# Two weight loads of the last expert split into 112 rows and two times eight rows

## What is computed

```
xe = h[idx]                                   # 16 experts x 32 tokens x 2048
hid = silu(xe @ w_gate) * (xe @ w_up)         # w_gate, w_up: 16 x 2048 x 1024
ye = (hid @ w_down) * gates                   # w_down: 16 x 1024 x 2048
h_lat = h_lat + mod * combine(idx, ye)        # then the final RMS norm
```

## Time and profile before

| | |
|---|---|
| median of three runs | 1685.66 us |
| the profiled execution | 1684.07 us |
| its span, first to last instruction | 1682.1 us |
| busy share of the span: PE, DVE, ACT, POOL | 86%, 42%, 19%, 7% |
| mean rate of the DMA engines over the span | 352 GB/s |
| chain that ended last | PE 57%, DMA 35%, DVE 4% |

### The profile page before, as it was taken

How to read it: one execution, slowest core, us unless ns; L and a number is a source line. 1 busy time by engine, 2 the same in 40 slices (tenths; PEclk the granted TensorE clock), 3 DMA queues, 4 the chain that set the end, 5 groups by cost and what they waited for, 6 DMA issues and landing times.

```text
span 1682.1 us, 19830 instructions
## 1 busy us (share of the span) xinstructions
PE 1451.6 (86%) x8030; PEld 867.9 (52%) x8030; DVE 712.0 (42%) x1149; ACT 327.7 (19%) x572; POOL 121.9 (7%) x106
## 2 busy tenths in 40 slices
PE   8999999999999998989878787766787776886786
PEld 6678778878888777875313241221332132332232
DVE  4446777678767876662222122112221211411122
ACT  3333333233333345530000000000000000000001
POOL 0000000004322243001000000000000000000002
PEclk8999999999999999999978888888888878878899
DMA  9996658657746764599999999999999999999997
GB/s 397 420 421 234 230 200 300 225 206 253 266 144 257 271 229 175 184 416 428 428 425 429 428 427 428 427 428 429 416 415 428 428 427 428 427 427 429 427 427 293
DMA packets 55404, 592.00 MB, mean 352 GB/s; under 512 B 6284, under 2 KB 6412, under 8 KB 7576
## 3 DMA queue, kind: packets, MB, share of 16 engines
q1 hardware_dynamic: 54008, 584.61, 85.0%
q10 hardware_dynamic: 1312, 6.16, 1.0%
HBM read 588.65 MB, written 2.10 MB: 351 GB/s over the span
## 4 chain that ended last, share of the span: by engine, by line
PE 57%; DMA 35%; DVE 4%; issue 2%; ACT 1%; POOL 0%; SPq 0%; DVEq 0%; POOLq 0%; ACTq 0%
DMA ring<-in_w_up 18%; DMA ring<-in_w_down 15%; PE bank L630 8%; PE bank L632 8%; PE bank L631 8%; PE bank L981 6%; PE bank L917 4%; PE bank L626 3%; PE bank L627 2%; PE bank L896 2%; PE bank L628 2%; PE bank L950 2%; PE bank L580 2%; PE bank L884 2%; DMA ring<-in_w_down_last 2%
## 5 line engine op out<-in xcount | busy, mean ns | idle before, releaser
L981 PE MATMUL bank<-ring,xg 128*32 128x512 f32 x1504 | 217.7, 707 | 122.5 <-DMA ring<-in_w_up 90.5
L1414 DVE TENSOR_TENSOR whl<-ring,whl 128x512 fp32r<-128x512 f32 x276 | 208.6, 759 | 131.1 <-ACT whl L1081 130.2
L1081 ACT ACTIVATE whl<-ring 128x512 fp32r<-128x512 f32 x276 | 173.4, 630 | 266.9 <-PE bank L632 219.4
L630 PE MATMUL bank<-whl,uh 128*128 128x512 f32 x512 | 206.5, 403 | 1.6 <-DVE vv L1443 0.7
L632 PE MATMUL bank<-whl,ul 128*128 128x512 f32 x512 | 199.8, 390 | 0.0
L631 PE MATMUL bank<-whl,uh 128*128 128x512 f32 x512 | 199.5, 390 | 0.0
L981 PEld LDWEIGHTS bank<-ring,xg 128*32 128x32 f32 x1504 | 45.0, 119 | 273.8 <-DMA ring<-in_w_up 140.7
L1397 DVE SCALAR_TENSOR_TENSOR part<-ring,csT,part 128x1024 f32<-128x1024 f32 x104 | 140.5, 1351 | 0.1
L896 PE MATMUL bank<-yy,gcur 128*128 128x512 f32 x252 | 132.9, 654 | 4.9 <-DVE yy L1708 3.5
L1280 ACT ACTIVATE gup<-bank 128x512 f32<-128x512 f32 x32 | 18.7, 597 | 593.5 <-PE bank L981 593.5
L1760 DVE COPY gup<-bank 128x512 f32<-128x512 f32 x32 | 22.0, 689 | 238.4 <-PE bank L981 238.4
(11 more groups left out here) (264 smaller groups left out, 1625.5 us busy)
## 6 DMA issues: line engine op xcount, KB each, us to landing
ring<-in_w_up SPq DMA_DIRECT2D x61, 2048.0 KB, 25.7
ring<-in_w_gate SPq DMA_DIRECT2D x33, 2048.0 KB, 25.7
ring<-in_w_mod_b SPq DMA_DIRECT2D x63, 1024.0 KB, 5.1
ring<-in_w_down SPq DMA_DIRECT2D x30, 2048.0 KB, 27.3
ring<-in_w_in SPq DMA_DIRECT2D x53, 1024.0 KB, 4.9
ring_b<-in_w_gate SPq DMA_DIRECT2D x15, 2048.0 KB, 20.5
ring_c<-in_w_gate SPq DMA_DIRECT2D x15, 2048.0 KB, 23.7
ring<-in_w_mod_a SPq DMA_DIRECT2D x28, 1024.0 KB, 16.1
```

The lines of the kernel that those rows point to most:

```text
L630: mm(ps, hi[:, k, cols], wh, start=k == 0, stop=False)
L981: last = mm(bank[2 * m + half][32 * kk:32 * kk + 32, :], xg[:, 4 * j + kk, CAP * ei:CAP * ei + CAP], parts[kk // of][0][:, kk % of, 512 * ...
L1081: a(whl[:, cidx % (AHEAD + 1), 0, :], slot_buf(slot[n])[:, 512 * (k % 4):512 * (k % 4) + 512], ACT.Copy).then_inc(hi_split, 1)
L1414: v.tensor_tensor(whl[:, cidx % (AHEAD + 1), 1, :], slot_buf(slot[n])[:, 512 * (k % 4):512 * (k % 4) + 512], whl[:, cidx % (AHEAD + 1), 0, ...
```

## The change

Items 6 and 7 of the last expert are no longer one transfer of 128 rows each. Each is issued as three transfers behind one wait: rows 0 to 111, rows 112 to 119, rows 120 to 127. All three add 16 to the semaphore of the same buffer, and the count that TensorE waits for before it uses the item is 32 higher. The bytes, their places in memory and the sources are the same.

```diff
+SHARED_ROWS = ((0, 112), (112, 120), (120, 128))
...
-        return pair_buf(d), ring_full[2 * d], g * (16 * 8) + (fills[2 * d] + 16 * (2 * ei + n // RING + 1))
+        more = 16 * (len(SHARED_ROWS) - 1) if is_final(g, ei) and i in (6, 7) else 0
+        return pair_buf(d), ring_full[2 * d], g * (16 * 8) + (fills[2 * d] + 16 * (2 * ei + n // RING + 1) + more)
...
         for i in range(6, 8):
             sp.wait_ge(moe_used, 12 * (E - 1) + i - RING + 1)
-            expert_item(E - 1, i, i - 4)
+            d = moe_pairs[(i - 4) % RING]
+            for r0, r1 in SHARED_ROWS:
+                sp.dma_start(pair_buf(d)[r0:r1, :], w_up[E - 1, i % 4][r0:r1, :]).then_inc(ring_full[2 * d], 16)
```

## The result

The change makes the kernel slower: 1704.72 us (median of five runs, 1700.63 to 1704.95) against 1685.66 us, ratio 1.0108 with a 95% interval of 1.0097 to 1.0119, so 19 us more. The forecast was 1691.0 and a range up to 1698. The profiled execution is the quickest of the five, 1700.63 us with a span of 1698.8, 16.7 us above the span before; the other four took 1704.56 to 1704.95, and what they lose beyond it stands in no trace.

A forecast was written before the change was run, and what follows sets the result against it. The last landing of `w_down` plus a fixed 14.75 us tail bounds the kernel. Leading engines become 8.6 us later over two items, less their 3.3 us lead: 1685.66 + 5.3 = 1691.0 us; forecast's own range 1689 to 1698, full range from 1683.8.

The forecast's parts named there:

- What bounds the kernel: End of the span: the last piece of `w_down` lands at 1667.35, and the end follows 14.75 us later.
- Four more issues cost nothing: SyncE, items 6 and 7: 0.7 us more issuing per item, covered by the full queue; cost 0, without cover 1.4 us.
- The 112-row transfers: Items 6 and 7: seven rows per engine instead of eight, 0.61 us less per item, no extra; upper bound 0.6 us extra.
- The eight-row transfers on the leading eight: Items 6 and 7: small transfers go to the eight engines that finish early, one row each, judged by the four-row transfer.
- the rival that put the small transfers on the lagging group: Items 6 and 7: engines that finish late get nine rows, 1.2 us later, 1686.9 us; chance 0.03.
- the balance: Rival: eight rows land side by side, so the last landing comes 1.2 us earlier, 1684.4 us; chance 0.31.
- The lead of 3.3 us: At the last landing: eight engines finish at least 3.3 us ahead; subtracted from their 8.6 us delay, giving +5.3 us.
- Four rows in a line: Each eight-row transfer takes four rows' time, 2.4 us; a chosen middle between 0.61 and 4.9 us.
- What would show it: Signs: DMA share well under 1.00 about 1643 to 1658, last landing 1671 or later, microseconds of wait before item 7.
- Item 7 doesn't set the end: TensorE after item 7: it lands up to 5.3 us later, but the chain has 3.7 us to spare and the last piece slips equally.
- the toll: Rival: small transfers of 1.9 to 3.2 rows, or slow 112-row part; 0 to 3 us slower, some 1687; chance 0.08.
- One engine for all eight rows: Rival: one engine gets all rows of each small transfer, 18 us in all, 1700 us or above; chance 0.02.

The follow-up runs named there:

- The cut by columns: Items 6 and 7 as three transfers each of all 128 rows (3584, 256 and 256 elements), against the kernel before: 1686.23 against 1684.92 us, ratio 1.0007.
- the halves: Items 6 and 7 each as two transfers of 64 rows, against the kernel before: 1700.54 against 1684.92 us, ratio 1.0091.
- the probe: Kernel before plus one eight-row transfer of 2 KB rows behind the four-row one, GpSimd waiting for both: 1685.21 against 1685.50 us, ratio 0.9999.
- the crossed pair: Kernel before plus four eight-row transfers: scattered rows into adjoining partitions, 1695.93 us; adjoining rows into every fourth partition of 0 to 31, 1686.48; against 1685.50.
- the run with four rows: Kernel before plus four additional four-row transfers into every fourth partition of 64 to 79, behind items 6 and 7: 1687.90 against 1685.39 us, ratio 1.0018.

## Why the prediction was wrong

- **What bounds the kernel: right.** The last landing plus an unchanged tail, 14.77 us against 14.75.
- **Four more issues cost nothing: right.** The cut by columns has them, ratio 1.0007 (0.9997 to 1.0017).
- **The 112-row transfers: the step that failed.** "I take no extra", with 0.6 us per item as the upper bound. By difference they cost some 10 us for the two items: of the 19, four eight-row transfers beside whole items account for 9.5, if the two costs add up. The cut into 112 and 16 rows loses 16.3, and the halves lose 15.6 with no small transfer at all, at half the rate. The 112-row transfer never ran without small ones beside it, so its share is worked out and not measured. The bound assumed that one row in seven has to wait. Why 112 rows come down to about half the rate, as two halves do, no row shows; how their rows are dealt to the engines is not in the traces. I had written that full rate needs each engine on partitions of its own, and used it for the eight rows only. It bears on the 112 as well.
- **The eight-row transfers on the leading eight: wrong.** The inference from four rows to eight did not hold; the probe's 1653.20 shows it. So the rival that put the small transfers on the lagging group was right of some of their engines, and the balance could not work as drawn: it adds rows to engines that lag.
- **The lead of 3.3 us: wrongly subtracted.** The sum has the leading group use up its lead and become the lagging one. In the trace after, the four-row transfer's engines and the last landing are late by the same amount, 16.6 and 16.7 us. The loss fell on both groups, and no lead can absorb such a loss.
- **Four rows in a line: the size fits, the mechanism is not shown.** By themselves, with no lead, four transfers of four rows come to 16 x 0.61 = 9.8 us; 9.5 and 10.4 were measured for adjoining partitions. But the same count gave 2.4 us for rows apart from each other on paths in use, and 7.9 were measured. So the agreement may be luck.
- **The rule that sets the path.** By the Trainium skill (SBUF — State Buffer, section "Door 1: The DMA port swizzle") the partition number picks one of sixteen ports of some 27 GB/s each, and rows 0 to 63 reach only eight of them. The halves' 206 to 220 GB/s agree (8 x 27 = 216, an estimate from that page's figure), and that the partition written to decides in the crossed pair agrees, too. I had used the rule for the small transfers only. The Trainium skill's advice for two partition halves, in DMA: Bandwidth & Descriptors ("Rules for kernel authors"), is one 128-partition transfer. It was right for the halves, and the runs put a price on it: 15.6 us for two items of 2 MB, and 19 us for the cut of this change.
- **What would show it: half wrong.** I said the DMA share would fall well under 1.00. It stayed at 0.93 to 1.09, and the rate fell. Late items and the steeper wait for item 7 (7.45 us against 0.18) came as said.
- **Item 7 doesn't set the end: nearly wrong.** TensorE's granted clock was 0.50 (its level of 1.2 GHz) from 1645 to 1650, behind the wait of 3.97 us, and 0.55 from 1660 to 1665, in the wait of 7.45 us; the earlier trace rows had 1.00. Before the change it waited 3.7 us for pieces; after it, 1.1 us:

```profile
PE bank L936 <- DMA ring<-in_w_down_last: 1.1, 1, 1.1
```

A little more, and the end would have hung on TensorE, as in the run with four rows.
- **The rivals.** The balance (1684.4) and the toll (1687) fell. "One engine for all eight rows" came nearest in time, 1700 or above, for a reason that isn't needed: 15.6 us are lost without any eight-row transfer. The top of the forecast's own working, 1700.7 with all eight rows in a line and no extra on the 112, lies under the measured 1704.72, too, so it was not the choice of four rows in a line that put the sum too low.

## What to carry to other kernels

Before a full-height load is cut by rows, ask for each piece which partitions its engines write at the same moment, not only how many rows each engine gets: here a cut into equal halves, the same number of rows for every engine, ran at half the rate. A cut by columns cost nothing that could be told. And look at the rate in GB/s beside the busy share of the DMA engines; the share stayed near 1.0 here while the rate was halved. Compare an early item in both traces, too: here 2.0 of the 16.7 us between them were there before the first changed transfer was issued.

## What was not expected of the hardware

- The whole item ahead of a split one lands late, too: item 5, untouched, made TensorE wait 3.97 us.
- The engines of the four-row transfer kept their lead through the loss (late by 16.6 us, the last landing by 16.7).
- One split item cost 10.8 us and two 19 us.
- The four-row transfer landed with the leading engines (1649.13), the eight-row one behind it 4.1 us later (1653.20).
- Four additional transfers of eight rows apart from each other cost 1.5 us into partitions 0 to 31, within the noise, and 7.9 us into 64 to 95.
- The two halves ran at 206 to 220 GB/s, half of 428: if sixteen engines then share eight paths, a path carries no more for two engines than for one.
- An issue of eight rows at every fourth partition took SyncE about 0.67 us from one to the next, twice the 0.34 us of a 128-row issue. Two issues of eight adjoining rows took 0.69 us together.
